# Query projection from raw tokens with quartered weights, and half of the router logits folded into the last output sum

## The chip, the cores and the metric

The kernel runs on one core of one Trainium2 chip. The metric is the device time of one execution in microseconds (us), median of the runs. Engines are named as in the profile: PE is TensorE (PEld its weight loads), DVE is VectorE, ACT is ScalarE, POOL is GpSimd, SP is SyncE, which issues most transfers.

## What is computed

One block over 256 tokens of width 1024, all in float32:

```
h = rmsnorm(x, mix_norm_g)
proj = h @ w_in                        # [u_pool | q | k | v | gates], 512 columns each, gates 2 x 1024
q = apply_partial_rotary(rmsnorm(q, q_norm_g), cos, sin)     # per head of 64
k = apply_partial_rotary(rmsnorm(k, k_norm_g), cos, sin)
o = diff_attention(q, k, v, lam) ; o = rmsnorm(o, subln_g) * (1.0 - lam_init)
merged = g_pool * y_pool + g_attn * (o @ attn_up)
x = x + merged @ w_out
h2 = rmsnorm(x, ffn_norm_g)
logits = h2 @ router_w + router_b      # 32 experts, top 4, softmax over the four
x = x + sum over the experts of comb[:, e] * expert_e(h2)    # each with three 1024 x 1024 weights
```

## The kernel before

Activations are held transposed, channels on the 128 partitions in 8 chunks; tokens are two tiles t = 0, 1 of 128. The front's weights come as pieces of 2 MB (1024 x 512 floats) in the order Q, K, V, U, two gate pieces, `pool_up`, two gate pieces, `attn_up`, two halves of `w_out`. They land in four slots of a ring (`LAND`). Four more slots hold the rounded high part of a piece: except for Q, every product is done as three fp32r matmuls (`mm3`, L509 to L511) of a high part that ACT writes (`hi_part`, L840) and a low part that DVE writes (`lo_part`, L1085), in quarters. Q is multiplied in plain fp32 (L548), 8 chunks for each token tile.

Each engine works through its own program in order, written by hand, with semaphores between them. SP issues x (L441), five small vectors as rows (L443), Q, nine parameter tensors (L447, `par_in`), then K, V and U (L450), and later pieces as slots come free. PE first transposes the row vectors (L523, waits for all five), and, when DVE has scaled the tokens by their norm (L1067, `h_ready`), transposes the tokens (L529). DVE multiplies by the norm's gain on the way out of PSUM (L1079, `hT_ready`). Then PE does Q. ACT casts h (L850), then the K piece (L840), and only then copies and squares the first Q strip (L862, L865), which gives its PSUM bank free for K (`strip_free0`). DVE makes the low parts of h and of K, then per strip of Q and K the head norm and the rotary (L1114 to L1128), with the low parts of V between and those of U behind. PE transposes Q and K (L562) when both are ready.

Attention, gates and `w_out` follow. The four sums of `w_out` go in the order (tile 0, half 0), (1, 0), (0, 1), (1, 1) (`project`), with DVE adding each to x (L1228) and PE turning it (`turn_half`, L687). Behind the last sum PE computes the router's logits, tokens on partitions, 32 columns (`token_logits`, L693): channels 0 to 3 for both tiles, then channels 4 to 7. `keep_clock` (L699) are matmuls whose results nobody reads. DVE takes the logits, picks four experts and builds the tables. Then the loop over 32 experts runs, six pieces of 2 MB each through the ring's eight slots (issued at L476, multiplied at L780); the first eight are issued as `w_out` and the pieces ahead of it leave the slots, and the ninth waits for the first piece of the loop to be done (`piece_done`).

Of the kernel before, what the change touches and what calls it, by code (L numbers as in the profile page):

```python
# [20 lines left out]
ALU = mybir.AluOpType  # L21
ACT = mybir.ActivationFunctionType
AX = mybir.AxisListType
# [39 lines left out]
R_MIXG, R_BGATE, R_PSCALE, R_SUBLN, R_FFNG, R_ROWS = 0, 8, 24, 28, 29, 37  # L63
# [20 lines left out]
def build(nc, A, consts, out):  # L84
    with ExitStack() as ctx:
# [21 lines left out]
        ident = con[:, C_IDENT:C_IDENT + P]  # L107
        iota = con[:, C_IOTA:C_IOTA + BLOCK]
# [40 lines left out]
        squares = prob.rearrange("p b m s -> p b (m s)")  # L149

# [43 lines left out]
        ranks = part(NT * E).rearrange("p (t e) -> p t e", t=NT)  # L194
        junk2 = (actT.rearrange("p c h s -> p (c h s)"),
# [24 lines left out]
        phalf = small[:, 240:244]  # L220
        oss = small[:, 152:160]
# [30 lines left out]
        rows_in = sem("rows_in")  # L252
        gain_in = sem("gain_in")
# [9 lines left out]
        h_ready = sem("h_ready")  # L263
# [46 lines left out]
        x2T_last = sem("x2T_last")  # L310
        zero_row = sem("zero_row")
# [185 lines left out]
        def _(pe):  # L497
# [34 lines left out]


            pe.wait_ge(cols_ready, 1)
            for i, piece in enumerate((Q_P, K_P, V_P)):
                for t in range(NT):
# [3 lines left out]
                    if piece == Q_P:  # L540
                        piece_wait(piece)
                        pe.wait_ge(hT_ready, 2 * t + 2)
# [129 lines left out]

            def project(t, half):
                for m in range(NC):
# [713 lines left out]
```

## Time and profile before

| | us |
|---|---|
| median of 3 runs (lowest, highest) | 1107.81 (1107.04, 1108.08) |
| the profiled execution's own time | 1109.42 |
| its span, first to last instruction | 1107.6 |
| PE busy / DVE busy / ACT busy | 1059.0 / 274.4 / 188.4 |
| moved by the DMA engines | 432.94 MB |

The profiled execution lies 1.6 us above the median; its span is what the rows divide. Of the span about 185 us are the front, and the rest is the loop over the experts. Busy time of PE holds overlapping matmuls, so it says little about waits.

### The profile page before, as it was taken

To read this page: it belongs to the slowest core of one execution; us is meant where nothing else is said; L and a number is where in the kernel's file an instruction comes from. 1 tells how busy PE (TensorE), PEld (TensorE's weight loads), DVE (VectorE), ACT (ScalarE), POOL (GpSimd) and SP (SyncE) were. 2 spreads that over 40 slices of the span, in tenths; PEclk is the share of its full clock that TensorE was granted. 3 is DMA by queue.
4 is the path that set the end of the run, shared out by engine and by line. 5 is a ranking of instruction groups with operands and counts; after the bars stand their busy time and mean duration, and the time that the engine had idled before them with its cause. 6 is when DMAs were issued, how large, how long until landed. Compare 5 with 4: busy or idle time off the path is not lost.

```text
span 1107.6 us, 12567 instructions
## 1 busy us (share of the span) xinstructions
PE 1059.0 (96%) x5116; PEld 450.4 (41%) x5116; DVE 274.4 (25%) x557; ACT 188.4 (17%) x339; POOL 29.9 (3%) x43
## 2 busy tenths in 40 slices
PE   6999999999999999999999999999999999999998
PEld 3889985333333333333333333333333233333332
DVE  4976564111111111111111111111111111111112
ACT  4556532110100010001000100001000000010000
POOL 0070020000000000000000000000000000000000
PEclk9999999999999999999999999999999999999999
DMA  9725596999999999999999999999999999999995
GB/s 312 267 100 191 189 370 273 414 430 425 430 428 427 428 430 428 427 429 429 428 428 430 429 428 428 430 429 427 428 430 429 427 428 430 428 427 428 430 428 237
DMA packets 43918, 432.94 MB, mean 391 GB/s; under 512 B 5973, under 2 KB 6522, under 8 KB 19322
## 3 DMA queue, kind: packets, MB, share of 16 engines
q1 hardware_dynamic: 43482, 432.39, 93.4%
q10 hardware_dynamic: 416, 0.28, 0.1%
q8 instruction: 13, 0.21, 0.1%
q14 instruction: 7, 0.06, 0.0%
HBM read 431.61 MB, written 1.05 MB: 391 GB/s over the span
## 4 chain that ended last, share of the span: by engine, by line
PE 47%; DMA 42%; DVE 7%; ACT 2%; SPq 1%; issue 1%; DVEq 0%; ACTq 0%
PE ps L780 32%; DMA ring<-in_exp_w_up 22%; DMA ring<-in_exp_w_gate 19%; PE ps L509 2%; PE ps L511 2%; PE ps L510 2%; PE ps L752 2%; PE ps L745 2%; DVE ring_r L1085 2%; PE ps L786 2%; DVE arena L1353 2%; DVE arena L1351 1%; ACT ring_r L840 1%; SPq L447 1%; DMA ring<-in_w_in 1%
## 5 line engine op out<-in xcount | busy, mean ns | idle before, releaser
L780 PE MATMUL ps<-ring,arena 128*64 128x512 f32 x3072 | 688.7, 596 | 24.8 <-DMA ring<-in_exp_w_gate 21.0
L780 PEld LDWEIGHTS ps<-ring,arena 128*64 128x64 f32 x3072 | 210.5, 137 | 442.3 <-issue 383.0
L1341 DVE TENSOR_SCALAR arena<-ps 128x512 f32<-128x512 f32 x32 | 22.1, 691 | 476.4 <-PE ps L780 476.4
L1351 DVE TENSOR_SCALAR arena<-ps 128x512 f32<-128x512 f32 x32 | 22.1, 691 | 235.4 <-PE ps L780 235.4
L992 ACT COPY arena<-ps 128x512 f32<-128x512 f32 x32 | 18.8, 589 | 319.3 <-PE ps L739 319.3
L752 PE MATMUL ps<-arena 64*128 64x512 f32 x264 | 65.6, 615 | 0.8 <-ACT arena L998 0.8
L990 ACT ACTIVATE arena<-arena 128x512 f32<-128x512 f32 x32 | 20.1, 629 | 259.2 <-DVE arena L1341 259.2
L739 PE MATMUL ps<-arena 128*64 128x512 f32 x264 | 63.2, 600 | 0.1
L509 PE MATMUL ps<-ring_r 128*128 128x256 f32 (+1 forms) x192 | 59.3, 309 | 2.2 <-ACT arena L865 1.5
L998 ACT COPY arena<-ps 128x512 f32<-128x512 f32 x32 | 18.7, 585 | 235.0 <-PE ps L780 235.0
L510 PE MATMUL ps<-ring_r 128*128 128x256 f32 (+1 forms) x192 | 57.7, 301 | 0.0
L511 PE MATMUL ps<-ring_r 128*128 128x256 f32 (+1 forms) x192 | 57.6, 300 | 0.0
L1085 DVE TENSOR_TENSOR ring_r<-ring,ring_r 128x1024 fp32r<-128x1024 f32 x44 | 54.2, 1279 | 8.9 <-ACT ring_r L840 8.7
L786 PE MATMUL ps<-arena_r 128*128 128x512 f32 x96 | 48.1, 501 | 1.4 <-issue 0.7
L745 PE MATMUL ps<-con,arena 128*128 128x128 f32 x260 | 40.8, 280 | 5.6 <-DVE arena L1353 5.5
L840 ACT CAST ring_r<-ring 128x1024 fp32r<-128x1024 f32 x44 | 43.6, 1051 | 12.9 <-DMA ring<-in_w_in 9.1
L745 PEld LDWEIGHTS ps<-con,arena 128*128 128x128 f32 x260 | 28.8, 140 | 34.1 <-DVE arena L1353 33.6
L786 PEld LDWEIGHTS ps<-arena_r 128*128 128x128 f32 x96 | 17.9, 186 | 58.6 <-issue 50.3
L752 PEld LDWEIGHTS ps<-arena 64*128 64x128 f32 x264 | 22.8, 186 | 43.1 <-issue 43.1
L509 PEld LDWEIGHTS ps<-ring_r 128*128 128x128 f32 x192 | 36.5, 190 | 5.8 <-ACT arena L865 2.9
L511 PEld LDWEIGHTS ps<-ring_r 128*128 128x128 f32 x192 | 36.6, 190 | 1.3
L510 PEld LDWEIGHTS ps<-ring_r 128*128 128x128 f32 x192 | 36.6, 190 | 1.2
(183 smaller groups left out, 585.3 us busy)
## 6 DMA issues: line engine op xcount, KB each, us to landing
ring<-in_exp_w_gate SPq DMA_DIRECT2D x64, 2048.0 KB, 32.8
ring<-in_exp_w_up SPq DMA_DIRECT2D x64, 2048.0 KB, 35.3
ring<-in_exp_w_down SPq DMA_DIRECT2D x64, 2048.0 KB, 34.4
ring<-in_w_in SPq DMA_DIRECT2D x8, 2048.0 KB, 8.7
ring<-in_w_out SPq DMA_DIRECT2D x2, 2048.0 KB, 8.1
xt<-in_x SPq DMA_DIRECT2D x4, 512.0 KB, 6.8
ring<-in_pool_up SPq DMA_DIRECT2D x1, 2048.0 KB, 7.5
ring<-in_attn_up SPq DMA_DIRECT2D x1, 2048.0 KB, 7.4
```

The source lines that it names most:

```text
L509: mm(dst, a[0], b[1], start=start, stop=False)
L510: mm(dst, a[1], b[0], start=False, stop=False)
L511: return mm(dst, a[0], b[0], start=False, stop=stop)
L739: last = mm(ps[BLOCK * half:BLOCK * (half + 1), 6, :], pick[:, buf, t, :], h2[:, t, HALF * half:HALF * (half + 1)], start=(t == 0), stop=( ...
L745: last = tr(ps[:, bank, P * c:P * (c + 1)], src[:, P * c:P * (c + 1)], ident)
L752: last = mm(ps[:, 2 * t + half, :], pickT[rows, P * t:P * (t + 1)], y_e[rows, :], start=False, stop=True, skip_group_check=True)
L780: last = mm(ps[BLOCK * half:BLOCK * (half + 1), bank, :], src[:, c, k % 2, :], slot(n)[:, c, HALF * half:HALF * (half + 1)], start=False, ...
L786: mm(ps[:, bank, :], this_e[:, buf].rearrange("p h s -> p (h s)"), bias_rows[:, k, :], start=True, stop=False, skip_group_check=True)
L840: nc.scalar.copy(quarter(hi, q), quarter(ring[:, n % LAND, :], q)).then_inc(w_hi, 1)
L1085: return v.tensor_tensor(dst, whole_ap, hi.bitcast(F32), ALU.subtract)
L1351: v.tensor_scalar(u1, ps[:, 5, :], LIMIT, -LIMIT, ALU.min, ALU.max).then_inc(expert_step, 1)
L1353: v.scalar_tensor_tensor(out=act_out.rearrange("q (c p) -> q p c", c=4), in0=u1.rearrange("q (p c) -> q p c", c=4), scalar=1.0, in1=gs.rea ...
```

## The change

**Front.** x's first tile, the norm's gain alone, x's second tile and Q in four quarters lead SP's queue; K follows at once, and the nine parameters stand between K and V. The other four row vectors go by ACT's queue. PE starts with eight matmuls over a block of ones, then transposes the raw tokens as they land; Q is computed from tokens times gain, without the tokens' norm, whose factor cancels in the head norm if its epsilon is scaled (`qeps`). For everything else the normed h is made behind: DVE puts the norm's factors on a diagonal, PE multiplies ones by it to spread them over the partitions (`spread_norm`, in the middle of Q's first tile), and DVE multiplies (`h_normed`). DVE no longer scales x ahead of the transposes.

**Logits.** Channels 0 to 3 of the logits are now computed with experts on partitions, each channel chunk in its own 32 partitions of one PSUM bank, 256 tokens wide, within the last `w_out` sum (`early_logits`, ahead of its chunk m = 5). ACT copies the 128 x 256 block, and one matmul per token tile against four stacked identities (`four_rows`) adds the four partial sums into the logits' bank. One `keep_clock` matmul of two is gone between the later logits.

```diff
         @block.sync
-            for t in range(NT):
-                sp.dma_start(xt[:, t, :], A["x"][0, P * t:P * (t + 1), :]).then_inc(x_in[t], 16)
-            for r0, src in rows:
-                sp.dma_start(prow[r0:r0 + src.shape[0], :], src).then_inc(rows_in, 16)
+            sp.dma_start(xt[:, 0, :], A["x"][0, 0:P, :]).then_inc(x_in[0], 16)
+            r0, src = rows[0]
+            sp.dma_start(prow[r0:r0 + src.shape[0], :], src).then_inc(mix_in, 16)
+            sp.dma_start(xt[:, 1, :], A["x"][0, P:S, :]).then_inc(x_in[1], 16)
+            for q in range(3):
+                sp.dma_start(front_slot(Q_P)[:, 2 * q:2 * q + 2, :], front[Q_P][:, 2 * q:2 * q + 2, :]).then_inc(q_in[q], 16)
+            sp.dma_start(front_slot(Q_P)[:, 6:8, :], front[Q_P][:, 6:8, :]).then_inc(slot_in[Q_P % LAND], 16)
             for n, src in enumerate(front):
-                if n == 1:
+                if n == Q_P:
+                    continue
+                if n == V_P:
                     for dst, par in params:
                         sp.dma_start(dst, par).then_inc(par_in, 16)
...
         @block.tensor
+            pe.wait_ge(filler_ready, 1)
+            for _ in range(8):
+                mm(ps[:, 7, :], filler[:, 0:P], filler[:, P:P + HALF], start=True, stop=True)
             pe.wait_ge(con_in, 16)
-            pe.wait_ge(rows_in, 16 * 5)
-            tr(ps[:, 0, 0:R_ROWS], prow[0:R_ROWS, :], ident[0:R_ROWS, 0:R_ROWS]).then_inc(cols_T, 1)
-
-            for t in range(NT):
-                pe.wait_ge(h_ready, t + 1)
+            pe.wait_ge(mix_in, 16)
+            tr(ps[:, 6, 0:NC], prow[0:NC, :], ident[0:NC, 0:NC]).then_inc(cols_T, 1)
+            for t in range(NT):
+                pe.wait_ge(x_in[t], 16)
...
+            def spread_norm():
+                pe.wait_ge(rows_in, 16 * 4)
+                tr(ps[:, 1, R_BGATE:R_ROWS], prow[R_BGATE:R_ROWS, :],
+                   ident[R_BGATE:R_ROWS, R_BGATE:R_ROWS]).then_inc(cols_T, 1)
+                pe.wait_ge(diag_ready, NT)
+                for k in range(NT):
+                    last = mm(ps[:, 7, P * k:P * (k + 1)], ones_f, diag[:, k, :], start=True, stop=True)
+                last.then_inc(spread, 1)
...
                     for c in range(NC):
                         if piece == Q_P:
+                            if t == 0 and c == 4:
+                                spread_norm()
+                            if c % 4 == 0:
+                                pe.wait_ge(hT_ready, 2 * t + c // 4 + 1)
+                            if t == 0 and c % 2 == 0:
+                                q_wait(c // 2)
...
+            def early_logits():
+                pe.wait_ge(rw_ready, 1)
+                pe.wait_ge(x2T_even, 2)
+                for c in range(4):
+                    last = mm(ps[E * c:E * (c + 1), 4, 0:S], rw[:, c, :], x2T[:, c, :], start=True, stop=True)
+                last.then_inc(part_done, 1)
...
+                    if t == 1 and half == 1 and m == 5:
+                        early_logits()
...
-            pe.wait_ge(rw_ready, 1)
-            pe.wait_ge(x2T_even, 2)
-            token_logits(0, 0)
-            token_logits(1, 0)
+            pe.wait_ge(part_moved, 1)
+            for t in range(NT):
+                mm(ps[:, 5 + t, 0:E], part_logit[:, P * t:P * (t + 1)], four_rows, start=True, stop=False)
             turn_half(1, 1)
             pe.wait_ge(x2T_odd, 1)
             token_logits(0, 1)
-            keep_clock(2, 6)
+            keep_clock(1, 4)
...
         @block.vector
+            v.memset(filler.bitcast(F32), 1.0).then_inc(filler_ready, 1)
...
-                v.tensor_scalar(xt[:, t, :], xt[:, t, :], rstd[:, t:t + 1], None, ALU.mult).then_inc(h_ready, 1)
...
+            for t in range(NT):
+                v.tensor_scalar(diag[:, t, :], ident, rstd[:, t:t + 1], None, ALU.mult).then_inc(diag_ready, 1)
...
+                    v.tensor_tensor(h_normed[place], hT[place], wide(ps[:, 7, P * t:P * (t + 1)], [P, 4, P], 1),
+                                    ALU.mult).then_inc(normed_T, 1)
```

PE's first instructions, before. The names in brackets are the semaphores that a row waits for.

```order
L523 MATMUL ps<-con,arena 128x37 [waits rows_in,con_in]
L529 MATMUL ps<-con,xt 128x128 [waits h_ready]
L529 MATMUL ps<-con,xt 128x128 x7
L529 MATMUL ps<-con,xt 128x128 [waits h_ready]
L529 MATMUL ps<-con,xt 128x128 x7
L548 MATMUL ps<-ring,arena 128x512 [waits hT_ready,slot_in0,cols_ready]
L548 MATMUL ps<-ring,arena 128x512 x7
```

And the same place now:

```order
L546 MATMUL ps<-arena_r 128x512 x7
L549 MATMUL ps<-con,arena 128x8 [waits mix_in,con_in]
L554 MATMUL ps<-con,xt 128x128 [waits x_in0]
L554 MATMUL ps<-con,xt 128x128 x7
L554 MATMUL ps<-con,xt 128x128 [waits x_in1]
L591 MATMUL ps<-ring,arena 128x512 [waits q_in0,hT_ready]
L591 MATMUL ps<-ring,arena 128x512
L591 MATMUL ps<-ring,arena 128x512 [waits q_in1]
L591 MATMUL ps<-ring,arena 128x512
L560 MATMUL ps<-con,arena 128x29 [waits rows_in]
L564 MATMUL ps<-arena,con 128x128 [waits diag_ready]
L564 MATMUL ps<-arena,con 128x128
```

The transposes wait for x itself, Q waits for its first quarter, and three small instructions stand between Q's fourth and fifth chunk.

SP's queue, before:

```order
L450 DMA ring<-in_w_in 128x8x512
L447 DMA arena<-in_q_norm_g 128x64
L447 DMA arena<-in_k_norm_g 128x64
L447 DMA arena<-in_lambda_q 128x64 x2
L447 DMA arena<-in_lambda_k 128x64 x2
L447 DMA arena<-in_pool_w 128x4x128
L447 DMA arena<-in_router_w 128x8x32
L447 DMA arena<-in_router_b 128x32
L450 DMA ring<-in_w_in 128x8x512 x3
```

The first of these is Q and the last are K, V and U. Now:

```order
L463 DMA ring<-in_w_in 128x2x512 x3
L464 DMA ring<-in_w_in 128x2x512
L473 DMA ring<-in_w_in 128x8x512
L470 DMA arena<-in_q_norm_g 128x64
L470 DMA arena<-in_k_norm_g 128x64
L470 DMA arena<-in_lambda_q 128x64 x2
L470 DMA arena<-in_lambda_k 128x64 x2
L470 DMA arena<-in_pool_w 128x4x128
L470 DMA arena<-in_router_w 128x8x32
L470 DMA arena<-in_router_b 128x32
L473 DMA ring<-in_w_in 128x8x512 x2
```

K (the first 128x8x512) has moved ahead of the nine parameters.

PE behind the last sum of `w_out`, before (L687 turns x, L693 are logits, L699 is `keep_clock`):

```order
L687 MATMUL ps<-con,xt 128x128 [waits x2_ready]
L687 MATMUL ps<-con,xt 128x128 x3
L693 MATMUL ps<-arena 128x32 [waits x2T_even,rw_ready,zero_row]
L693 MATMUL ps<-arena 128x32 x7
L687 MATMUL ps<-con,xt 128x128 [waits x2_ready]
L687 MATMUL ps<-con,xt 128x128 x3
L693 MATMUL ps<-arena 128x32 [waits x2T_odd]
L693 MATMUL ps<-arena 128x32 x3
L699 MATMUL ps<-arena_r 128x512 x2
L693 MATMUL ps<-arena 128x32 [waits x2T_last]
L693 MATMUL ps<-arena 128x32 x3
```

Now, from the place within the sum:

```order
L720 MATMUL ps<-arena 32x256 [waits x2T_even,rw_ready]
L720 MATMUL ps<-arena 32x256 x3
...
L739 MATMUL ps<-con,xt 128x128 [waits x2_ready]
L739 MATMUL ps<-con,xt 128x128 x3
L764 MATMUL ps<-arena 128x32 [waits part_moved,zero_row]
L764 MATMUL ps<-arena 128x32
L739 MATMUL ps<-con,xt 128x128 [waits x2_ready]
L739 MATMUL ps<-con,xt 128x128 x3
L745 MATMUL ps<-arena 128x32 [waits x2T_odd]
L745 MATMUL ps<-arena 128x32 x3
L751 MATMUL ps<-arena_r 128x512
L745 MATMUL ps<-arena 128x32 [waits x2T_last]
```

Eight small logit matmuls behind the sum have become four wide ones within it (nine matmuls of the sum stand between) and two behind it.

## Rows read from the trace of the kernel before

**Rows 1.** The page: GB/s moved, in 40 slices of 27.7 us.

```profile
GB/s 312 267 100 191 189 370 273 414 430 425 430 428 427 428 430 428 427 429 429 428 428 430 429 428 428 430 429 427 428 430 429 427 428 430 428 427 428 430 428 237
```

**Rows 2.** Windows behind the logits: engines' busy us, granted clock, DMA share, GB/s.

```profile
179.00:182.00 3.00, 2.90 (x7) 0.98 (x8) 2.74 (x17) 0.00 (x0) 0.00 (x0) 0.50 1.01 431
184.00:189.00 5.00, 4.28 (x21) 1.74 (x23) 0.69 (x1) 1.28 (x1) 0.00 (x0) 1.00 0.01 2
```

**Rows 3.** Timeline of SP's queue: start, us taken to issue, what.

```profile
8.79 4.83 SPq L447 DMA_DIRECT2D arena<-in_router_b  x1
13.66 25.41 SPq L450 DMA_DIRECT2D ring<-in_w_in  x5
...
171.73 0.80 SPq L476 DMA_DIRECT2D ring<-in_exp_w_gate  x2
189.41 3.76 SPq L476 DMA_DIRECT2D ring<-in_exp_w_up  x2
```

**Rows 4.** Timeline of PE in the front: start, us, what.

```profile
7.37 0.29 PE L523 MATMUL ps<-con,arena 37*128 37x37 f32 x1 [7.37 <-DMA arena<-in_ffn_norm_g]
8.69 3.33 PE L529 MATMUL ps<-con,xt 128*128 128x128 f32 x16 [1.03 <-DVE xt L1067]
12.04 13.97 PE L548 MATMUL ps<-ring,arena 128*128 128x512 f32 x32
...
27.49 0.50 PE L509 MATMUL ps<-ring_r 128*128 128x512 f32 x1 [1.48 <-ACT arena L865]
...
49.86 1.91 PE L562 MATMUL ps<-con,xt 128*128 128x128 f32 x16
```

**Rows 5.** Windows of the front, columns as in rows 2.

```profile
0.00:5.00 5.00, 0.00 (x0) 0.00 (x0) 0.06 (x1) 1.52 (x3) 1.29 (x10) 1.00 0.65 217
5.00:11.00 6.00, 2.60 (x12) 2.49 (x13) 3.39 (x12) 2.87 (x7) 0.40 (x1) 1.00 1.05 386
27.50:38.50 11.00, 11.00 (x48) 8.92 (x48) 9.94 (x28) 5.90 (x10) 0.00 (x0) 1.00 0.95 352
```

**Rows 6.** Timeline of ACT in the front.

```profile
4.97 1.06 ACT L828 ACTIVATE arena<-xt 128x1024 f32<-128x1024 f32 x1 [1.81 <-DMA xt<-in_x]
...
22.57 3.88 ACT L840 CAST ring_r<-ring 128x1024 fp32r<-128x1024 f32 x4 [9.08 <-DMA ring<-in_w_in]
...
26.84 0.59 ACT L865 ACTIVATE arena<-ps 128x512 f32<-128x512 f32 x1
```

**Rows 7.** Timeline of DVE in the front and behind the last sum.

```profile
9.97 1.42 DVE L1079 TENSOR_TENSOR arena<-ps,cols 128x512 f32<-128x512 f32 x2
...
23.65 4.63 DVE L1085 TENSOR_TENSOR ring_r<-ring,ring_r 128x1024 fp32r<-128x1024 f32 x4 [8.40 <-ACT ring_r L840]
...
49.52 4.62 DVE L1085 TENSOR_TENSOR ring_r<-ring,ring_r 128x1024 fp32r<-128x1024 f32 x4
...
174.35 0.69 DVE L1257 COPY arena<-ps 128x512 f32<-128x512 f32 x1 [1.93 <-PE ps L687]
```

**Rows 8.** The chain that ended last, behind the last sum and in the loop.

```profile
171.70 0.44 PE ps L687 x4
172.13 1.71 PE ps L693 x16
173.84 0.47 PE ps L687 x4
174.31 0.81 PE ps L693 x8
175.12 0.54 PE ps L699 x2
175.66 0.82 PE ps L693 x8
...
180.36 2.82 PE ps L739 x8
...
194.72 0.43 PE ps L786
195.15 7.04 PE ps L780 x32
```

More of the change, by code:

```diff
@@ L194, in build @@
         ranks = part(NT * E).rearrange("p (t e) -> p t e", t=NT)
+        taken[0] = max(taken[0], places["bias_raw"] + 3 * HALF)
+        four_rows = part(E)
+        part_logit = pickw[:, 0].rearrange("p t h s -> p (t h s)")
         junk2 = (actT.rearrange("p c h s -> p (c h s)"),
@@ L220, in build @@
         phalf = small[:, 240:244]
+        var = small[:, 244:246]
+        qeps = small[:, 246:248]
         oss = small[:, 152:160]
@@ L252, in build @@
         rows_in = sem("rows_in")
+        mix_in = sem("mix_in")
+        q_in = [sem(f"q_in{q}") for q in range(3)]
+        mix_ready = sem("mix_ready")
+        diag_ready = sem("diag_ready")
+        filler_ready = sem("filler_ready")
+        spread = sem("spread")
+        normed_T = sem("normed_T")
         gain_in = sem("gain_in")
@@ L262, in build @@
         x_std = sem("x_std")
-        h_ready = sem("h_ready")
         h_T = sem("h_T")
@@ L539, in _ @@
                     tokens = slice(P * t, P * (t + 1))
-                    if piece == Q_P:
-                        piece_wait(piece)
-                        pe.wait_ge(hT_ready, 2 * t + 2)
+                    if piece == Q_P and t == 1:
+                        pe.wait_ge(cols_ready, 1)
                     elif piece == K_P and t == 0:
@@ L692, in token_logits @@
                 for c in range(4 * q, 4 * q + 4):
-                    last = mm(ps[:, 4 + t, 0:E], x2T[:, c, P * t:P * (t + 1)], rw[:, c, :],
-                              start=(c == 0), stop=(c == NC - 1))
+                    last = mm(ps[:, 5 + t, 0:E], x2T[:, c, P * t:P * (t + 1)], rw[:, c, :],
+                              start=False, stop=(c == NC - 1))
                 return last
@@ L716, in _ @@
             token_logits(0, 1)
-            keep_clock(2, 6)
+            keep_clock(1, 4)
             pe.wait_ge(x2T_last, 1)
             token_logits(1, 1).then_inc(logit_done, 1)
-            keep_clock(3, 6)
+            keep_clock(3, 4)
             for b in range(4):
@@ L820, in _ @@
             act.dma_start(con[:], consts).then_inc(con_in, 16)
+            for r0, src in rows[1:]:
+                act.dma_start(prow[r0:r0 + src.shape[0], :], src).then_inc(rows_in, 16)
             act.dma_start(gain[:], A["ffn_norm_g"].rearrange("l (h p c) -> p (l h) c", h=2, p=P)).then_inc(gain_in, 16)
@@ L973, in _ @@
             root2(0)
+            act.wait_ge(part_done, 1)
+            nc.scalar.copy(part_logit, ps[:, 4, 0:S]).then_inc(part_moved, 1)
             act.wait_ge(x2_T, 3)
@@ L1082, in _ @@
                                     ALU.mult).then_inc(hT_ready, 1)
+            dve.wait_ge(x_std, NT)
+            own(v.reciprocal(rstd, rstd))
+            for t in range(NT):
+                v.tensor_scalar(diag[:, t, :], ident, rstd[:, t:t + 1], None, ALU.mult).then_inc(diag_ready, 1)
+            dve.wait_ge(x_var, NT)
+            own(v.tensor_scalar(qeps, var, EPS, None, ALU.mult))
+            dve.wait_ge(cols_T, 2)
+            v.tensor_copy(cols[:, R_BGATE:], ps[:, 1, R_BGATE:R_ROWS]).then_inc(cols_ready, 1)
+            dve.wait_ge(cols_ready, 1)
+            v.tensor_scalar(hgate, cols[:, R_BGATE:R_BGATE + 2 * NC], 0.5, None, ALU.mult)
+            v.tensor_scalar(phalf, cols[:, R_PSCALE:R_PSCALE + NG], 0.5, None, ALU.mult)
+            own(v.tensor_scalar(subln8, cols[:, R_SUBLN:R_SUBLN + 1], 0.5 * (1.0 - LAM_INIT), None, ALU.mult))
+            dve.wait_ge(hT_ready, 2 * NT)
+            dve.wait_ge(spread, 1)
+            for t in range(NT):
+                for q in range(2):
+                    place = (slice(None), slice(4 * q, 4 * q + 4), slice(P * t, P * (t + 1)))
+                    v.tensor_tensor(h_normed[place], hT[place], wide(ps[:, 7, P * t:P * (t + 1)], [P, 4, P], 1),
+                                    ALU.mult).then_inc(normed_T, 1)
             def minus(dst, whole_ap, hi):
@@ L1114, in _ @@
                 own(v.tensor_reduce(qss[:, i, :], squares[:, i % 2, :].rearrange("p (g d) -> p g d", d=HD), AX.X, ALU.add))
-                v.tensor_scalar(qrs[:, i, :], qss[:, i, :], 1.0 / HD, EPS, ALU.mult, ALU.add).then_inc(qk_var, 1)
+                if w == 0:
+                    v.scalar_tensor_tensor(out=qrs[:, i, :], in0=qss[:, i, :], scalar=1.0 / HD,
+                                           in1=qeps[:, t:t + 1].broadcast_to([P, 8]), op0=ALU.mult,
+                                           op1=ALU.add).then_inc(qk_var, 1)
+                else:
+                    v.tensor_scalar(qrs[:, i, :], qss[:, i, :], 1.0 / HD, EPS, ALU.mult, ALU.add).then_inc(qk_var, 1)
                 dve.wait_ge(qk_std, i + 1)
@@ L1262, in _ @@
             for t in range(NT):
-                last = v.scalar_tensor_tensor(out=logit[:, t, :], in0=ps[:, 4 + t, 0:E],
+                last = v.scalar_tensor_tensor(out=logit[:, t, :], in0=ps[:, 5 + t, 0:E],
                                               scalar=rstd[:, t:t + 1], in1=rb, op0=ALU.mult, op1=ALU.add)
```

38 lines of the change are left out of this document (21 added, 17 removed).

## The prediction, made before the changed kernel ran

> **What bounds the kernel now.** I read the rate of the transfers over the whole span first, because the kernel moves 433 MB. From the eighth slice on the core moves 425 to 430 GB/s without a pause [rows 1], so the loop over the experts is bound by its weight stream, and work of the engines inside it is hidden. Next the stretch ahead of the loop, at the stream's own start: at 184 to 189 us the DMA engines move 2 GB/s [rows 2]. All eight slots are full. The last two of them were issued at 171.73, right behind the last sum of `w_out`, and the ninth piece could only be issued at 189.41, when PE had used up the first one [rows 3]. So the end of the kernel is the moment at which PE frees the first slot, plus a stream of fixed length, plus a fixed tail. What PE gains ahead of the loop comes out whole at the end, as long as more than 5 us of idle DMA stand there; and since the last prefetch hangs on the last `w_out` sum, it moves along with a gain from further in front.
>
> Then PE's way to the loop. In the front, PE waits to 7.37 for the row vectors, transposes from 8.69, starts Q at 12.04 behind its own transposes and ends it at 26.01. Then it stands still until 27.49 for ACT's L865 [rows 4]. That one is late because ACT first casts the K piece, which landed only at 22.57, and then copies and squares, to 27.43 [rows 6]. K landed late because SP held its issue back to 13.66, the last parameter alone taking 4.83 us to issue [rows 3]. From 27.5 PE is full, 11.00 of 11 us, and DVE nearly (9.94) [rows 5]. DVE's chain from its low parts of K (start 23.65, end 28.28) to those of U at 49.52 is almost without gaps, and PE's transposes at 49.86 hang on both [rows 7, 4]. So a gain has to reach PE's start of K and DVE's end with K's low parts. Behind the last sum, PE's rows follow each other without a gap from 171.70 to 176.48 [rows 8].
>
> **The front, step by step.** *Q's start.* x's first tile (0.52 MB) was there at 4.97 [rows 6]; with the constants 0.80 MB were wanted by then, and 5.0 us at 217 GB/s are 1.085 MB moved. So a landing is seen about 0.28 MB, or 0.7 us at 386 GB/s, after its bytes have had their turn [rows 5]. Q's first quarter ends at 0.80 + 0.52 + 0.52 = 1.85 MB: 5 + 0.765/0.386 + 0.7 = 7.7 us. The tokens are ready by then: the gain vector now stands right behind x's first tile, say 5.5; its transpose and copy, four transposes at 0.21 (3.33/16 [rows 4]) and one DVE product of 0.71 (1.42/2 [rows 7]) end near 7.4. x's norm, its scaling and the other row vectors are no longer ahead. So Q starts at 7.7 instead of 12.04. The later quarters come 1.35 us apart (0.52/0.386), PE takes 1.75 for two chunks, so they don't hold it.
>
> *Q's end.* 13.97 us as before [rows 4], plus the three small instructions in its middle, 0.5 us (three transposes' worth, 0.1 to 0.2 each). The diagonal that they wait for needs ACT's second square and DVE's four products; by the same row lengths that is near 10.4, before PE wants it at 11.2. End: 7.7 + 13.97 + 0.5 = 22.2.
>
> *K.* Now right behind Q: bytes to 5.53 MB, 5 + 4.445/0.386 + 0.7 = 17.2 us instead of 22.57. ACT and DVE now also make and split the normed h, four DVE products of about 0.7 more, but that ends near 17.3, on DVE ahead of its first low part of K. From K's landing to the end of ACT's square were 4.86 us (22.57 to 27.43 [rows 6]): 22.1. PE starts K behind Q and behind that: 22.3 instead of 27.49, 5.2 us earlier. DVE starts 1.08 behind ACT as before: 18.3, ends at 22.9 instead of 28.28, 5.4 us earlier. The smaller, **5.2 us**, goes through to 49.86, and on from there, since later pieces wait for slots that come free earlier by the same.
>
> What hides the rest: the eight matmuls over ones stand in time in which PE waited anyway (until 7.37). The memset for them (640 columns) is DVE's only work then. The parameters land later, behind K. Before, Q's bytes had had their turn at 5 + 2.345/0.386 = 11.1 us and K's began at 22.57 - 0.7 - 5.4 = 16.4, so parameters and the late issue held the queue for at most 5.3 us. Now that comes behind K's bytes (16.5): at most 21.8, seen at 22.5, and DVE asks for them at 22.9. V is behind them, 5.4 us more and the lag: 27.9, and ACT casts V only after its second head root, at about 28.5 (DVE's chain moved by 5.4). Both covers are thin, half a us. If they are gone, each us of lateness costs at most one.
> Bounds of the front: if clock, gain vector or queue make Q start 1.5 us later and the params come 0.5 us late, 3.2; if Q starts as soon as the tokens can be, with K's landing as limit, 5.5.
>
> **The logits.** Removed behind the sum: 12 of 16 records (16 fp32 records in 1.71 us, 0.107 each; the two group matmuls are 4 records): 1.28 us. One `keep_clock`: 0.27. Together 1.55 us [rows 8]. The new order needs: turning 0.44, group 0.43, turning 0.47, logits 0.81, `keep_clock` 0.27. DVE's copy of the last quarter (0.69, started 0.5 behind the start of its turning [rows 7, 8]) ends 2.1 us behind the sum and PE comes to it at 2.4, so it is hidden, by 0.3 us. ACT's added copy of 128 x 256 falls in the sum's last chunks, 9 matmuls or 2.1 us long, on an idle ACT.
>
> Added within the sum, on PE's path: 4 matmuls of 256 columns, 8 records. The nearest row is the experts' L780, where neighbours go to two halves of the columns: 32 records of 512 in 7.04 us, 0.22 each [rows 8], while a record with the whole width took 0.437 (13.97/32 [rows 4]). So neighbours in different columns do overlap, but the two records of one fp32 matmul don't. For 256 columns a record alone is 0.22; in four strips, issued in order, only the last record of one matmul and the first of the next overlap: 5 x 0.22 = 1.1 us. And the change of shape: a 128 x 128 matmul ahead of L780 takes 0.43 to its follower [rows 8], in K's strips it is 0.229 (11.00/48 [rows 5]), so 0.2 for a switch, 0.4 for in and out. Sum 1.5. Bounds: 0.44 if the four overlap wholly and switches are free; 2.2 if none overlaps (8 x 0.22 + 0.4). Net of the logits: 1.55 - 1.5 = **0.05 us**, bounds -0.65 and +1.1.
> The Trainium skill (TensorEngine Tiling (Array Packing), Key Properties) says that changing the tiling mode drains TensorE; the 0.2 us of the row agrees. Its TensorE: Matmul & The Clock Gate (The mechanism, Part 3) has tiles overlapping to the duration of one matmul plus some 4 ns each; by that the four would cost about 0.45 and the net would be near +0.7, and the row's 0.22 for a half-width record speaks for less overlap in fp32.
>
> **The sum.** 5.2 + 0.05 = 5.25 us. The profiled execution would go from 1109.42 to 1104.2; against the median of the runs, which is 1.6 lower, 1107.81 - 5.25 = **1102.6 us**.
>
> **Rivals.**
> *Thin covers break* (chance 0.16): parameters or V land 2 us later than worked out, because many small packets stand behind K and SP's issue of V sits behind them. For it: the 4.83 us issue. Against: the 5.3 us are an upper bound, since SP's own lateness is in them. DVE's head norm of Q then starts late and PE waits at 49.86 - 5.2: gain 3, 1104.8 us.
> *Nothing arrives* (0.07): another stretch between 50 and 170 us is tied to something that doesn't move. Against: transfers there wait for PE's slots, and the stream has 5 us of slack. Gain under 2.2, about 1107.5.
> *Slower* (0.05): Q runs at the lower clock. The transposes before Q ran at 0.21 each, those at 171.70 at 0.11, so PE was at 1.2 GHz up to 12.0 and at 2.4 behind, though the granted clock's column shows 1.00 for both [rows 4, 5, 8]. Now PE has work from about 1.5, pauses near 5 and, after the transposes, near 7.5. If the clock is not up, or falls, each us of Q's work costs one more; from 5.3 us of such work on the kernel is slower, and with all 14 it would be 1116. Against: 3.3 us of transposes alone were enough before. The Trainium skill (TensorE: Matmul & The Clock Gate, Part 4) says that transposes don't count as busy for that clock; the trace before, with full speed right behind them, does not show this.
> *More* (0.08): the clock stood at 0.50 in 179 to 182 and the gather took 2.82 us [rows 2, 8]. If it now doesn't fall there, up to 1 us is won, and as much from the strips if they overlap wholly: gain 7, 1100.8. That it falls earlier would cost the same, and is within the range.
> *The forecast* (0.64): gain 3.7 to 6.5, 1101.3 to 1104.1.
>
> **How the numbers follow.** What a measurement of this kernel can tell from no change is 0.2%, 2.2 us. Faster by more: forecast, thin covers for the most part, and more: 0.86. Within: 0.08. Slower: 0.06. The range leaves out half of "more", nothing arrives and slower: 1100.4 to 1105.8.
>
> **What would show it.** Right: Q's first matmul at 7.3 to 8.3, K's at about 22.3, ACT's cast of K at about 17.2, transposes of Q and K at 44.7, the first piece of the loop freed at about 184.2, then an unbroken stream. The strips of logits: eight records in 1.0 to 1.2 us with 0.2 at each side. Wrong: Q's records at 0.85 instead of 0.43; a wait of DVE on the parameters or of ACT on V; PE waiting on ACT's L917 although K landed early; the time from the last sum's end to the logits' end not shrinking from 4.8 to about 3.2.

## The result, and the profile after

| | before | changed |
|---|---|---|
| median of the runs, us (lowest, highest), 5 of each | 1108.08 (1107.04, 1109.2) | 1101.92 (1100.92, 1102.93) |
| ratio, 95% interval | 1 | 0.9944 (0.9932 to 0.9956) |
| span of the profiled execution | 1107.6 | 1099.1 |

The changed kernel is 6.2 us faster; forecast were 5.25, within 1100.4 to 1105.8. The profiled execution of before lay above its median and that of the changed kernel below it, so the spans differ by more, 8.5 us. I first divide these 8.5 by place, and then sort out what is the change and what is the execution.

The page of the changed kernel, GB/s in 40 slices:

```profile
GB/s 315 292 112 161 231 394 298 419 428 427 427 429 429 429 429 428 429 429 428 428 428 428 428 429 429 429 429 428 429 429 427 428 429 428 428 429 429 429 428 253
```

The loop's stream is as unbroken as in [rows 1]. So the question is only when it becomes continuous, at the ninth piece. SP's queue in the front and around that point:

```profile
4.05 1.16 SPq L473 DMA_DIRECT2D ring<-in_w_in  x1
5.25 3.83 SPq L470 DMA_DIRECT2D arena<-in_q_norm_g  x1
...
15.21 3.26 SPq L470 DMA_DIRECT2D arena<-in_router_b  x1
18.51 1.54 SPq L473 DMA_DIRECT2D ring<-in_w_in  x2
...
166.84 0.81 SPq L499 DMA_DIRECT2D ring<-in_exp_w_gate  x2
182.27 3.76 SPq L499 DMA_DIRECT2D ring<-in_exp_w_up  x2
```

K's piece is issued at 4.05, the last prefetch 4.9 us earlier than in [rows 3] and the ninth piece 7.1 us earlier (182.27 against 189.41). PE in the front and from within the last sum on:

```profile
1.63 3.78 PE L546 MATMUL ps<-arena_r 128*128 128x512 f32 x8 [1.63 <-DVE arena_r L1114]
5.54 1.34 PE L554 MATMUL ps<-con,xt 128*128 128x128 f32 x8
7.50 1.09 PE L554 MATMUL ps<-con,xt 128*128 128x128 f32 x8 [0.61 <-DMA xt<-in_x]
8.97 3.67 PE L591 MATMUL ps<-ring,arena 128*128 128x512 f32 x8 [0.38 <-DMA ring<-in_w_in]
...
13.29 10.46 PE L591 MATMUL ps<-ring,arena 128*128 128x512 f32 x24
23.49 0.50 PE L532 MATMUL ps<-ring_r 128*128 128x512 f32 x1
...
163.57 0.40 PE L534 MATMUL ps<-ring_r,arena_r 128*128 128x512 f32 x1
163.90 0.64 PE L720 MATMUL ps<-arena 128*32 128x256 f32 x8
164.47 0.50 PE L532 MATMUL ps<-ring_r,arena_r 128*128 128x512 f32 x1
164.81 0.39 PE L533 MATMUL ps<-ring_r,arena_r 128*128 128x512 f32 x1
...
166.65 0.60 PE L739 MATMUL ps<-con,xt 128*128 128x128 f32 x4
...
170.03 0.94 PE L751 MATMUL ps<-arena_r 128*128 128x512 f32 x3
...
174.07 1.94 PE L790 MATMUL ps<-arena 128*64 128x512 f32 x8 [0.70 <-DVE arena L1360]
```

K starts at 23.49, 4.00 us earlier than in [rows 4]. The profile shows no idle time ahead of it, but only because the modelled ends of Q's records reach over its start; what held it is read from ACT below. The early logits are the eight records at 163.90. From L534 at 163.57 to the second matmul behind them, L533 at 164.81, are 1.24 us where two neighbours are 0.46 apart, so they cost 0.78. From the turning at 166.65 to the last `keep_clock` group at 170.03 are 3.38 us; before, the same two points were 171.53 and 176.31, 4.78 us. And the gather now ran at full clock in 1.94 us, against 2.82 in [rows 8].

ACT and DVE in the front:

```profile
14.31 2.41 ACT L902 CAST ring_r<-arena 128x512 fp32r<-128x512 f32 x4 [5.26 <-DVE arena L1147]
18.57 3.88 ACT L892 CAST ring_r<-ring 128x1024 fp32r<-128x1024 f32 x4 [1.85 <-DMA ring<-in_w_in]
22.36 0.57 ACT L914 COPY xt<-ps 128x512 f32<-128x512 f32 x1
22.84 0.59 ACT L917 ACTIVATE arena<-ps 128x512 f32<-128x512 f32 x1
```

```profile
19.65 4.63 DVE L1151 TENSOR_TENSOR ring_r<-ring,ring_r 128x1024 fp32r<-128x1024 f32 x4 [1.17 <-ACT ring_r L892]
24.20 0.19 DVE L1170 TENSOR_SCALAR arena<-arena 128x64 f32<-128x64 f32 x1
```

K landed 4.0 us earlier than in [rows 6], and ACT's square ended at 23.43, just ahead of PE's start of K: ACT's chain from K's landing still bounds it, as before (4.92 us from the first cast to PE's start in both). DVE followed 1.08 behind, and L1170 asked for the parameters without a wait. The windows of the transfers (columns as in [rows 2]):

```profile
0.00:5.00 5.00, 3.37 (x8) 2.48 (x8) 0.65 (x2) 1.62 (x3) 1.29 (x10) 1.00 0.63 196
5.00:11.00 6.00, 5.01 (x23) 3.19 (x23) 3.59 (x11) 2.55 (x6) 0.40 (x1) 1.00 1.02 377
```

The 8.50 us of the two spans by place, each a difference of two rows: K's start, -4.00 (27.49 to 23.49). From there to the turning behind the last sum, 144.04 to 143.16, -0.88. From there to the last `keep_clock` of the logits, -1.40. On to the ninth piece, 13.10 to 12.24, -0.86, all of it the gather. From the ninth piece to the end, 918.19 to 916.83, -1.36. The second of them is odd: 0.78 us of work were added there and yet it is shorter, so some 1.7 us had come from a place that the change doesn't name. Three theories for it (the letters are those of the expectations):

- **Execution.** It differs from one execution to the next.
- **E, lead.** It is the change's own doing: DVE enters K with more lead over PE, and later waits shrink.
- **C, place.** It is where the operands lie. The rows' layout grew from 37 to 61 columns (`R_ROWS`), `cols` with it by 96 bytes per partition, and everything behind it, the arena with the activations' high and low parts above all, moved by 96 bytes.

Of the other letters in the expectations, A is the prediction's own view, that PE's start of K and nothing behind it carries the front's gain, and F that the matmuls over ones buy nothing.

### The profile page after: what moved, and what is told of

Same layout as the page of the kernel before. It is cut to its first block, busy times and chain, and to the rows that moved or that the text cites. A ratio compares the mean times of both kernels' runs of the same rounds, so it can differ in the third digit from the quotient of the medians.

```text
span 1099.1 us, 12598 instructions
## 1 busy us (share of the span) xinstructions
PE 1058.1 (96%) x5124; PEld 449.3 (41%) x5124; DVE 276.5 (25%) x564; ACT 188.8 (17%) x340; POOL 30.2 (3%) x43
## 4 chain that ended last, share of the span: by engine, by line
PE 50%; DMA 39%; DVE 7%; ACT 2%; issue 1%; SPq 0%; DVEq 0%; ACTq 0%
PE ps L831 35%; DMA ring<-in_exp_w_up 19%; DMA ring<-in_exp_w_gate 19%; PE ps L803 3%; PE ps L532 2%; PE ps L534 2%; PE ps L533 2%; PE ps L796 2%; PE ps L837 2%; DVE arena L1425 2%; DVE ring_r L1151 2%; DMA ring<-in_w_in 1%; DVE arena L1423 1%; ACT ring_r L892 1%; PE ps L855 0%
## 5 line engine op out<-in xcount | busy, mean ns | idle before, releaser
L533 PE MATMUL ps<-ring_r 128*128 128x256 f32 (+1 forms) x192 | 57.7, 300 | 0.0
L534 PE MATMUL ps<-ring_r 128*128 128x256 f32 (+1 forms) x192 | 57.6, 300 | 0.0
L534 PEld LDWEIGHTS ps<-ring_r 128*128 128x128 f32 x192 | 36.6, 191 | 1.3
L533 PEld LDWEIGHTS ps<-ring_r 128*128 128x128 f32 x192 | 36.6, 191 | 1.2
```

Of the source, the lines that this page charges most:

```text
L533: mm(dst, a[1], b[0], start=False, stop=False)
L534: return mm(dst, a[0], b[0], start=False, stop=stop)
```

## Experiments

For each kernel two numbers are read from PE's timeline: the start of K's first matmul, and the distance from it to the turning behind the last sum. All of them:

| kernel | arena at byte | K starts | K to last sum | gather |
|---|---|---|---|---|
| before | 159200 | 27.49 | 144.04 | 2.82 |
| before again | 159200 | 26.99 | 144.04 | 2.91 |
| before, 32 bytes more | 159232 | 27.10 | 143.69 | 3.49 |
| before, 96 bytes more | 159296 | 27.09 | 142.38 | 1.94 |
| before, parameters late | 159200 | 26.78 | 142.31 | 3.08 |
| logits only | 159200 | 27.30 | 144.82 | 3.51 |
| front only | 159296 | 23.52 | 142.36 | 3.02 |
| changed | 159296 | 23.49 | 143.16 | 1.94 |
| changed again | 159296 | 23.18 | 143.15 | 2.66 |
| changed, 32 bytes more | 159328 | 22.75 | 144.49 | 2.94 |
| changed, 128 bytes more | 159424 | 24.27 | 144.34 | 3.08 |
| changed, no ones | 159296 | 23.00 | 142.86 | 1.94 |
| changed, K in quarters | 159296 | 22.41 | 142.17 | 2.64 |

### Each half of the change alone, and both kernels again

Front only has all of the change but `early_logits`, its copy, the group matmuls and the one `keep_clock` less. Logits only is the reverse:

```diff
+                    if t == 1 and half == 1 and m == 5:
+                        early_logits()
...
-            token_logits(0, 0)
-            token_logits(1, 0)
+            pe.wait_ge(part_moved, 1)
+            for t in range(NT):
+                mm(ps[:, 5 + t, 0:E], part_logit[:, P * t:P * (t + 1)], four_rows, start=True, stop=False)
...
-            keep_clock(2, 6)
+            keep_clock(1, 4)
```

> The front of the change without its logits. Theory A (the front's gain is what PE's start of K gains, 4.0 us in the changed kernel's trace, and goes through): K's first matmul at about 23.5, the ninth piece of the expert stream issued 4 us earlier than before (185.4), time 4 us less (ratio 0.9964), perhaps up to 1.5 us more if matmuls in the middle run at the shorter spacing. Rival B (the front moves nothing at the end; the gain is the logits and the clock): ratio within 0.2% of 1.

> The logits part alone on the kernel before. Theory A: about 0.8 us less (1.4 less behind the sum, 0.6 more within it), and 0.9 us more if the gather now runs at the full clock: ratio 0.9985 to 0.9993. If the clock falls at 179 us as before, the gather takes 2.8 us as before and the gain is 0.8. Rival B (the logits are the main part): 2 us or more less, ratio 0.998 or lower.

> The kernel before, once more, unchanged, for a second trace. Theory A: K starts at 27.5 again, and the two traces show how much the stretches 100 to 160 us and the falling clock at 179 us differ from one execution to the next. If the spacing of the 256-column matmuls at 100 to 112 us (0.120 us) is the same again, the 0.113 us of the changed kernel is a property of the kernel; if it flips, it is chance. Ratio 1 within 0.1%.

> The changed kernel, once more, unchanged, for a second trace and times on the same chip as its parts. Theory A: ratio 0.994 to 0.995; K's start at 23.5 again; the middle's 1.4 us and the gather's 0.9 us are there again if they belong to the kernel, gone if they are chance.

Front only: 1103.35 us, ratio 0.9952 (0.9938 to 0.9966). Logits only: 1108.33, 0.9999 (0.999 to 1.0008). Before again: 1108.0, 1.0 (0.999 to 1.0009). Changed again: 1101.89, 0.9946 (0.9932 to 0.996). So the front makes nearly all of the gain. The execution is ruled out: both repeats give their kernel's distance from K to the last sum to 0.01 us. The two kernels with the changed front have the short distance, so it came with the front. The logits alone, PE's rows behind the sum:

```profile
172.12 0.60 PE L701 MATMUL ps<-con,xt 128*128 128x128 f32 x4
...
175.50 0.94 PE L713 MATMUL ps<-arena_r 128*128 128x512 f32 x3
...
179.56 3.51 PE L752 MATMUL ps<-arena 128*64 128x512 f32 x8 [0.74 <-DVE arena L1304]
```

172.12 to 175.50 is 3.38, as in the changed kernel, and 144.82 is 0.78 above 144.04. So the logits are worth 1.40 - 0.78 = 0.62 us by the rows. In this execution the gather, almost wholly at the low clock, took 3.51 and ate it; in the time of the runs 0.1% is too little to be seen. In the repeat of before Q took longer. Its rows, and behind them Q's first records again, up to 16 us, in the repeat and in the first execution:

```profile
8.70 3.67 PE L529 MATMUL ps<-con,xt 128*128 128x128 f32 x16 [0.94 <-DVE xt L1067]
12.17 15.12 PE L548 MATMUL ps<-ring,arena 128*128 128x512 f32 x32
```

```profile
12.17 4.39 PE L548 MATMUL ps<-ring,arena 128*128 128x512 f32 x7
```

```profile
12.04 4.53 PE L548 MATMUL ps<-ring,arena 128*128 128x512 f32 x10
```

15.12 us against 13.97 in [rows 4]: seven records up to 16 us instead of ten, because the first three were 0.74 to 0.91 apart and the others 0.43. So PE came up to 2.4 GHz only about 2.5 us into Q, and in the first execution half a us before Q (the last transposes 0.11 apart instead of 0.21, which is also why the sixteen took 3.33 instead of 3.67). This differs between executions: with before's order of the front, Q took 13.94 to 14.14 us in three and 14.84 to 15.20 in the other three. It cost nothing here: K started at 26.99, 4.92 behind ACT's first cast of K (22.07), so ACT's chain bound it and not Q.

### The arena's place

```diff
         cols = sb("cols", [P, R_ROWS])
+        sb("pad", [P, 8])
```

Nothing uses this tensor; it moves all that is allocated behind `cols`. It was put into both kernels with 32 bytes, then into before with 96 (`[P, 24]`), which puts its arena at the changed kernel's address, and into the changed kernel with 128 (`[P, 32]`).

> The kernel before with eight unused floats behind the vector columns, which moves everything behind them in SBUF, the arena with the attention's, the branches' and the merged operands above all, by 32 bytes: its start is then a multiple of 64 bytes, as in the changed kernel, where the longer columns do the same. Theory C (the 1.4 us in the middle come from the arena's place): the 256-column matmuls of the pooling and attention projections at 0.113 us instead of 0.120, those of the output sum at 0.229 instead of 0.234, the ninth piece of the stream 1.4 us earlier counted from K's first matmul (160.5 instead of 161.9), ratio about 0.9987. Rival D (they come from the shifted timing against transfers and other engines): spacing 0.120 and 161.9 as before, ratio 1.

> The changed kernel with the same eight floats: its arena then starts 32 bytes off a multiple of 64, as in the kernel before. Theory C: spacing back at 0.120 and 0.234, 1.4 us of the gain gone, ratio about 0.9958 instead of 0.9946. Rival D: nothing changes.

> The kernel before with an unused tensor of 96 bytes per partition behind cols, so that the arena stands at byte 159296 of a partition, where the changed kernel has it (159200 before, 159232 with 32 bytes, 159328 in the changed kernel with 32 bytes more). Theory C, the arena's place sets the spacing of the matmuls: 0.113 to 0.114 us between 256-column matmuls of the pooling projection and 0.229 between 512-column ones of w_out, as in the changed kernel, and about 1.4 us less than before (1106.6), with K's start, the logits' tail and the gather as before. Rival, the spacing comes from something else that the changed front part brings (when pieces land, what runs beside them): 0.118 to 0.120 and 0.233 to 0.234, and 1108.0 as before.

> The changed kernel with an unused tensor of 128 bytes per partition behind cols: the arena at byte 159424, 128 above the changed kernel's. If the place counts by its remainder by 128 (64 in the changed kernel; 96, 0 and 96 in the three slower-spaced kernels), the spacing stays at 0.113 to 0.114 and 0.229 and the time at 1101.9. If it is not a matter of that remainder, 0.118 to 0.120 and 0.233 and about 1.2 us more (1103.1).

Measured: before with 32 bytes 1108.01, ratio 0.9996 (0.9986 to 1.0006); changed with 32 bytes 1102.91, 0.9945 (0.9932 to 0.9958); before with 96 bytes 1106.83, 0.999 (0.9981 to 0.9999); changed with 128 bytes 1103.62, 0.9955 (0.9941 to 0.9968). The windows from 98 to 110 us, within the pooling projection for the most part, in this order: before, changed, before with 96 bytes, changed with 128 bytes.

```profile
98.00:110.00 12.00, 12.00 (x103) 12.00 (x102) 7.75 (x14) 8.83 (x11) 0.00 (x0) 1.00 0.46 176
```

```profile
98.00:110.00 12.00, 12.00 (x108) 12.00 (x107) 8.85 (x17) 8.82 (x10) 0.00 (x0) 1.00 0.47 182
```

```profile
98.00:110.00 12.00, 12.00 (x107) 12.00 (x107) 7.93 (x14) 8.47 (x11) 0.00 (x0) 1.00 0.47 176
```

```profile
98.00:110.00 12.00, 12.00 (x104) 12.00 (x103) 7.89 (x16) 8.40 (x10) 0.00 (x0) 1.00 0.47 176
```

PE is full in all four and at full clock, yet it puts 107 or 108 matmuls into the 12 us with the arena at 159296, and 103 or 104 elsewhere. One by one, with the start of each as the first number, before and then the changed kernel:

```profile
103.92 0.28 PE L510 MATMUL ps<-arena_r,ring_r 128*128 128x256 f32 x1
104.05 0.28 PE L511 MATMUL ps<-arena_r,ring_r 128*128 128x256 f32 x1
104.16 0.29 PE L509 MATMUL ps<-arena_r,ring_r 128*128 128x256 f32 x1
```

```profile
103.88 0.28 PE L533 MATMUL ps<-arena_r,ring_r 128*128 128x256 f32 x1
103.99 0.28 PE L534 MATMUL ps<-arena_r,ring_r 128*128 128x256 f32 x1
104.11 0.28 PE L532 MATMUL ps<-arena_r,ring_r 128*128 128x256 f32 x1
```

The spacing is 0.113 us in all six kernels with the arena at 159296, and 0.118 to 0.120 in the seven with it elsewhere, the one other edit of the front or not. C is borne out: the kernel before, with nothing but an unused tensor, has the changed kernel's distance (142.38 against 142.36 of front only), and the changed kernel loses 1.2 to 1.3 us with its arena moved (144.34 and 144.49 against 143.16). What in the address counts is open. It is not the remainder by 64 or by 128: 159232 is a multiple of 64 as 159296 is, and 159424 has the same remainder by 128, and neither has the short spacing. Both simple forms of C in the expectations have thus failed. In the time of the runs before with 96 bytes is 0.1% faster by the ratio, with an interval from nothing to 0.2%: 0.1 to 2.1 us, which holds the rows' 1.7 but would not have shown it. Nor do the times show the loss in the changed kernel with 32 bytes more: its ratio, 0.9945, is the changed kernel's. So C rests on the rows alone.

### Is DVE's lead worth something?

Before, with the parameters between K and V and nothing else changed:

```diff
-                if n == 1:
+                if n == V_P:
```

> The kernel before with one edit of the front: the nine parameter transfers behind K's piece. Theory A (PE's start of K sets the gain, and it needs both an earlier K and an earlier end of Q): K lands near 17 us, but Q ends at 26.0 as before, so K's first matmul is at 26.1 instead of 27.5 and the gain is 1.4 us, ratio 0.9987. Rival E (K's landing alone sets it, through DVE): 4 us or more, ratio 0.996.

1106.09 us, ratio 0.9975 (0.9966 to 0.9985). Its rows of ACT, DVE and PE:

```profile
17.36 3.88 ACT L840 CAST ring_r<-ring 128x1024 fp32r<-128x1024 f32 x4 [3.62 <-DMA ring<-in_w_in]
```

```profile
18.43 4.63 DVE L1085 TENSOR_TENSOR ring_r<-ring,ring_r 128x1024 fp32r<-128x1024 f32 x4 [2.95 <-ACT ring_r L840]
23.40 0.20 DVE L1104 TENSOR_SCALAR arena<-arena 128x64 f32<-128x64 f32 x1 [0.34 <-DMA arena<-in_router_b]
```

```profile
12.14 15.20 PE L548 MATMUL ps<-ring,arena 128*128 128x512 f32 x32
```

K's start moved little, to 26.78 and not to the 26.1 of view A: Q bounds it now, and Q took 15.20 here, with its first records at the lower clock as in the repeat. DVE however begins K's low parts 8.35 us ahead of PE's K instead of 3.84, and the distance to the last sum fell by 1.73, though the arena stands where it did. So E names a mechanism that exists: behind K, DVE is the engine that PE waits for. It isn't what shortened the changed kernel's middle, since there DVE's lead is 3.84 again (19.65 to 23.49). By the time of the runs the gain of 2.3 us lies between what A (1.4) and E (4 or more) gave; the rows' sum, 1.73 and 0.2 to 0.7 of K's start, agrees with it.

### No matmuls over ones

```diff
-            pe.wait_ge(filler_ready, 1)
-            for _ in range(8):
-                mm(ps[:, 7, :], filler[:, 0:P], filler[:, P:P + HALF], start=True, stop=True)
```

> The changed kernel without the eight matmuls over ones. Theory A: PE's clock then comes up later, at 8 to 9 us; the transposes take 0.2 us each again and Q's start may move from 9.0 to at most 10, Q's first records perhaps at 0.85 us: 0 to 2 us lost, ratio 0.9946 to 0.9964. Rival F (the landing of x and of Q's quarters covers the slow clock wholly): nothing lost. Rival G (the fillers are needed for all of Q): 5 us or more lost.

1101.76 us, ratio 0.9941 (0.9928 to 0.9955).

```profile
5.31 3.67 PE L551 MATMUL ps<-con,xt 128*128 128x128 f32 x16
8.78 3.66 PE L588 MATMUL ps<-ring,arena 128*128 128x512 f32 x8
```

Without the ones the transposes take 3.67 us instead of 2.43. Q follows them without a wait for its first quarter, so in this execution they held Q up: with x's second tile at about the same time (6.7), the kernel of the next section started Q at 8.19, 0.6 us earlier. It did not reach the end, because the end didn't hang on PE here (see K in quarters). Q's eight records take 3.66 as with the ones, so the clock was up. That is not sure to be so each time: before's front, with only transposes ahead of Q, made Q up to 1.2 us longer in half of its six executions, the first records at the lower clock, and in none of the six traces with the ones was that so. The times, 1100.1 to 1103.88 for this kernel, can't show a gain of that size; so F is neither shown nor excluded. PE had been idle and did nothing but transposes before Q, and Q ran at 2.4 GHz, which is at odds with the Trainium skill (TensorE: Matmul & The Clock Gate, Part 4: PE-mode transpose), by which transposes don't raise the clock; and at odds too with the first trace of before, where the transposes themselves went from 0.21 to 0.11 each; the measurement decides.

### K in quarters

The changed kernel, K's piece in four transfers with a semaphore each, so that ACT starts on the first quarter:

```diff
+                if n == K_P:
+                    for q in range(3):
+                        sp.dma_start(front_slot(n)[:, 2 * q:2 * q + 2, :], src[:, 2 * q:2 * q + 2, :]).then_inc(k_in[q], 16)
+                    sp.dma_start(front_slot(n)[:, 6:8, :], src[:, 6:8, :]).then_inc(slot_in[n % LAND], 16)
+                    continue
...
+                if n == K_P:
+                    if q < 3:
+                        act.wait_ge(k_in[q], 16)
```

> The changed kernel with K's piece loaded in four quarters, each with a semaphore of its own (the last on the piece's), as Q's is: ScalarE rounds K's first quarter when it has landed, not when the whole piece has. Theory A, the front is bound by TensorE's chain (transposes, Q) and not by K's landing any more: K's matmuls start at 23.5 as in the changed kernel and the time stays at 1101.9. Rival E, VectorE's lead is used later: ScalarE's first rounding of K moves from 18.57 to about 17, VectorE's low parts from 19.65 to about 18.7, K's matmuls start at 23.5 all the same, and the attention part ends 0.5 to 1.0 us earlier: 1101.0 to 1101.4, as with the kernel in which the parameters came late (0.9 at V's end and 2.1 to 2.7 at the end, for 4.8 us of lead).

1100.05 us, ratio 0.9929 (0.9916 to 0.9943), the lowest median of the study, though the interval overlaps that of the changed kernel. ACT, DVE and PE:

```profile
15.85 3.88 ACT L903 CAST ring_r<-ring 128x1024 fp32r<-128x1024 f32 x4
```

```profile
17.62 4.62 DVE L1162 TENSOR_TENSOR ring_r<-ring,ring_r 128x1024 fp32r<-128x1024 f32 x4
```

```profile
8.19 3.67 PE L597 MATMUL ps<-ring,arena 128*128 128x512 f32 x8 [0.33 <-DMA ring<-in_w_in]
...
22.41 0.80 PE L538 MATMUL ps<-ring_r 128*128 128x512 f32 x1
```

DVE's lead over PE's K grew from 3.84 to 4.79, by 0.95, and the distance to the last sum shrank from 143.16 to 142.17, by 0.99. The same holds in the small for the kernel without ones, where ACT's cast of K came 5.22 ahead of PE's K instead of 4.92, and the distance was 0.30 shorter. Both say the same thing when the distance is counted from DVE's first low part of K instead of PE's start of K. Without ones that row is

```profile
18.85 1.23 DVE L1148 TENSOR_TENSOR ring_r<-ring,ring_r 128x1024 fp32r<-128x1024 f32 x1 [0.57 <-ACT ring_r L889]
```

To the turning behind the last sum are then 147.00 us in the changed kernel (19.65 to 166.65), 146.99 in its repeat, 147.01 without ones (18.85 to 165.86) and 146.96 with K in quarters (17.62 to 164.58), though PE began K 3.84, 3.84, 4.14 and 4.79 behind DVE. So in this range PE's start of K decides nothing: the end follows DVE's start with K, and that follows K's landing and ACT's first cast. This refutes view A for the changed kernel. Only where the lead is large does PE count: 4.5 us more of it gave 1.73.

K's own start, 22.41, was 1.1 earlier than in the changed kernel. 0.8 of it is Q's earlier start in this execution; the other 0.3 comes from the edit, since ACT's square now ends at 20.7 and only Q bounds K. Measured from Q's first record, DVE starts K 9.43 us behind it instead of 10.68: by the rows the quarters are worth 1.25 us. In the other executions with the changed front K's start lay between 22.75 and 24.27, with the landing of x's second tile.

## Why the prediction was right, and where its terms were off

**What bounds the kernel: right.** The stream is unbroken from the ninth piece on and its length was 916.8 to 918.5 us in all thirteen profiles. What PE gained ahead of it came out at the end.

**The front: 5.2 forecast, 4.0 measured** (27.49 to 23.49, and 3.8 between the two repeats). The steps that were off are the landings, of Q's first quarter (*Q's start*, 8.97 instead of 7.7) and of *K* (18.57 instead of 17.2). By the section on K in quarters the second is the one that counted: DVE began K at 19.65 instead of the 18.3 forecast, 4.0 us earlier than before instead of 5.4. By the windows after, 0.98 MB were moved by 5.0 instead of 1.085, which is 0.3 us. The rest is the lag between a transfer's turn in the queue and its landing. I took 0.7 us from x's first tile. x's second tile had its turn at 5 + (1.33 - 0.98)/0.377 = 5.9 and was seen at 7.48; Q's first quarter at 5 + (1.85 - 0.98)/0.377 = 7.3 and 8.97; K at 17.1 and 18.57: a lag of 1.5 to 1.7. It may be that bytes of later transfers move ahead of the earlier one's last when more are issued at once; no run shows it. Nor is the lag a constant: with the same order of transfers Q started anywhere from 8.19 to 9.87 in the seven kernels with the changed front, 8.32 in one that differs only by 32 unused bytes. So part of the miss is this one execution. And *the tokens are ready by then* named only the first tile: PE's program has the second tile's transposes ahead of Q, so x's second tile (7.48, then 1.09 of transposes) stood only 0.4 us ahead of the quarter. *Q's end*, 14.47 us behind its start, was near: K came 14.22 behind Q's start where Q bounded it (no ones, quarters). In the changed kernel it came 14.52 behind, since ACT's square, at 23.43, ended 0.3 later than Q would have needed. The two chains end close together, as forecast, only both later.

**Thin covers: they held.** V and the parameters came in time: DVE's L1170 behind K's low parts had no wait on the parameters. In the kernel with only the parameters moved the wait was 0.34.

**The logits: 0.05 forecast, 0.62 measured.** Behind the sum 1.40 came instead of 1.55. The four strips cost 0.78 instead of 1.5: the eight records start in two groups of four:

```profile
163.89:163.93 0.04, 0.03 (x4) 0.03 (x5) 1.00 1.91 819
163.93:164.14 0.21, 0.21 (x4) 0.13 (x8) 1.00 1.09 468
164.14:164.17 0.03, 0.03 (x8) 0.00 (x0) 1.00 0.00 0
```

(PE's busy us and records, PEld's, clock and transfers, for L720 alone.) Four start within 0.02 us, the other four 0.24 behind, which is about one record's time (0.22). So the four strips run side by side, and it looks as if the two records of a matmul follow each other, though the trace doesn't say which record is whose. The failed step is my reading of L780, from which I concluded that in four strips only the last record of one matmul and the first of the next overlap. From the first strip to the next matmul of the sum are 0.57 us, and the spacing ahead of it and behind is 0.33 and 0.34 instead of 0.23, so a change of shape costs 0.1, and not the 0.2 that I took: 0.57 + 0.33 + 0.34 - 0.46 = 0.78. The Trainium skill (TensorE: Matmul & The Clock Gate, Part 3, The mechanism), by which four tiles take little more than one, was nearer: the estimate from it was 0.45 for the four, and the 0.57 agree better with that than with my 1.1.

**The arena's place: 1.7 us by the rows, not forecast.** No term of the sum looked at addresses. Without it the gain would have been 4.6 by the rows (4.00 + 0.62), and it was 5.4 and 5.0, not far from the 6.2, in the time of the changed kernel with 32 and with 128 bytes more. So the forecast came near partly because its errors offset each other: 1.2 too much for the front, 0.6 too little for the logits, and 1.7 that was not on the list; 5.25 - 1.2 + 0.6 + 1.7 is 6.35, against 6.2 measured.

**The rivals.** *Nothing arrives* and *slower* did not come: Q's records were 0.43 apart from the second on. The prediction's reason against *slower*, that 3.3 us of transposes alone had been enough before, was luck of that one trace: in three of the six executions with before's front they were not. *More* was half right: the strips did overlap, and in the profiled execution the clock did not fall at the gather. That is chance, though: of the thirteen profiles it fell in ten, whatever the kernel, and the gather took 1.94 in the other three. It makes up to 1.6 us between executions (1.94 to 3.51), and 0.7 between the two of the changed kernel.

## What to carry to other kernels

Take a queue's lag as a range, from more than one execution: the 0.7 us read from the first transfer of one trace was 1.5 to 1.7 in the changed kernel's, and between executions of one order landings moved by 1.7 us. Before two chains that end together are given one number, ask which of them the end follows; here it was DVE's start with K, and PE's start of K moved by 0.3 and by 1 us against it without a trace at the end. If an engine is nearly full behind the point where another waits (here DVE behind K), give it its input in smaller pieces: K in quarters gave 1.25 us by the rows for a few lines. And when an edit changes the size of a small tensor, everything allocated behind it moves; before a gain or loss of a per mille is put down to the edit, put the old layout back with an unused tensor and measure both.

## What the hardware showed that was not expected

- The spacing of back-to-back fp32r matmuls depends on where their operands lie in SBUF: with 256 columns 0.113 us with the arena at byte 159296 and 0.118 to 0.120 at 159200, 159232, 159328 and 159424; with 512 columns 0.229 against 0.232 to 0.234. No address rule could be made out.
- The issue of one small parameter can hold SP for 3 to 5 us (3.83 and 3.26 here), and which one it is changes with what is queued ahead of it.
- Four fp32 matmuls in four column strips of the array run side by side: of their eight records four start within 0.02 us and the other four 0.24 us behind, 0.64 us busy in all.
- The moment at which PE comes up to 2.4 GHz in the front differs between executions: Q's 32 records, with only transposes ahead of them, took 13.97 and 15.12 us in two executions of before, and 13.94 to 15.20 in all six with its front, the first ones 0.85 apart instead of 0.43 in the slower ones.
